# A hybrid mixer and mixture-of-experts block on one core: result rows ordered by expert index, and summed slot by slot

## The reference

```
def moe_ffn(h, w_router, b_router, w_gate_up, b_gate_up, w_down, b_down):
    logits = (hf @ w_router) + b_router
    top_logits, top_idx = lax.top_k(logits, TOP_K)      # 4 of 32 experts for each of 512 tokens
    top_w = jax.nn.softmax(top_logits, axis=-1)
    ...
    def expert_block(args):                             # gate/up, clamp, swiglu, down: a row of 1024 per choice
    ...
    y = jax.ops.segment_sum(ys * slot_w[:, None], slot_tok, num_segments=n_tok)
    return y
...
x = x + moe_ffn(h, ...)
return rmsnorm(x, norm_final_w)
```

## Time and profile before

| | us |
|---|---|
| median of 3 runs | 2107.06 |
| the three runs | 2105.13 to 2107.47 |
| the profiled execution | 2103.68 |
| its span in the trace | 2101.9 |
| PE busy | 1975.9 (94%) |
| DVE, ACT, POOL busy | 482.2, 329.9, 194.4 |
| granted TensorE clock, mean | 0.969 |

### The profile page before, as it was taken

The page is one execution under the profiler, slowest core; times in us unless marked ns, Lnnn a source line. Parts: engine busy times, 40 slices in busy tenths (PEclk is TensorE's granted clock), DMA queues, the critical chain, the costliest instruction groups (busy, mean ns, idle before and its releaser), DMA issues.

```text
span 2101.9 us, 42330 instructions
## 1 busy us (share of the span) xinstructions
PE 1975.9 (94%) x18196; PEld 899.5 (43%) x18196; DVE 482.2 (23%) x884; ACT 329.9 (16%) x614; POOL 194.4 (9%) x244
## 2 busy tenths in 40 slices
PE   6999999999999999957999999999999999999990
PEld 4445555455554444442434343434434343434340
DVE  1272553625522211220101010110101010110105
ACT  3122323323232000100001010100000010100001
POOL 0000010000100000030010111101010111101010
PEclk9999999999999999968999999999999999999995
DMA  6011111111102321346999999999999999999945
GB/s 248 20 41 46 41 56 31 41 46 41 41 21 104 108 84 64 130 166 233 379 386 391 378 386 390 383 397 377 395 380 394 381 396 381 392 392 380 391 170 216
DMA packets 77609, 488.61 MB, mean 232 GB/s; under 512 B 13780, under 2 KB 14312, under 8 KB 23232
## 3 DMA queue, kind: packets, MB, share of 16 engines
q1 hardware_dynamic: 68832, 470.76, 58.0%
q0 software_dynamic: 8704, 16.82, 2.4%
HBM read 478.53 MB, written 17.45 MB: 236 GB/s over the span
## 4 chain that ended last, share of the span: by engine, by line
PE 90%; DVE 5%; DMA 1%; issue 1%; DVEq 1%; ACT 1%; POOL 0%; SPq 0%; ACTq 0%; POOLq 0%
PE ps L968 31%; PE ps L525 17%; PE ps L986 16%; PE ps L520 15%; PE ps L733 2%; DVE arena L1358 2%; DVE arena L1355 2%; PE ps L997 1%; PE ps L953 1%; PE ps L963 1%; PE ps L979 1%; PE ps L845 1%; PE ps L840 1%; PE ps L820 0%; DMA arena<-expert_rows 0%
## 5 line engine op out<-in xcount | busy, mean ns | idle before, releaser
L968 PE MATMUL ps<-arena 128*32 128x512 f32 x6144 | 667.0, 594 | 0.0
L968 PEld LDWEIGHTS ps<-arena 128*32 128x32 f32 x6144 | 184.4, 110 | 464.6 <-issue 458.5
L525 PE MATMUL ps<-hT,arena 128*128 128x512 f32 x768 | 351.8, 601 | 7.9 <-DVE arena L1355 7.9
L986 PE MATMUL ps<-arena,hT 128*32 128x256 f32 x6144 | 338.1, 380 | 0.0
L1840 DVE TENSOR_SCALAR arena<-ps 128x768 f32<-128x768 f32 x32 | 30.6, 958 | 953.0 <-PE ps L968 953.0
L986 PEld LDWEIGHTS ps<-arena,hT 128*32 128x32 f32 x6144 | 184.8, 110 | 141.6 <-issue 1.1
L1037 ACT ACTIVATE arena<-ps 128x512 f32<-128x512 f32 (+4 forms) x144 | 87.5, 608 | 884.8 <-PE ps L953 696.7
L525 PEld LDWEIGHTS ps<-hT,arena 128*128 128x128 f32 x768 | 140.0, 192 | 154.8 <-issue 149.6
L1930 POOL DMA_INDIRECT expert_rows<-hT,six x96 | 95.8, 998 | 816.3 <-ACT hT L1037 769.3
L520 PE MATMUL ps<-arena 128*128 128x128 f32 (+3 forms) x480 | 142.0, 434 | 2.2 <-DVE arena L1355 2.2
L520 PEld LDWEIGHTS ps<-arena 128*128 128x128 f32 x480 | 77.4, 191 | 54.4 <-issue 47.1
(11 more groups left out here) (203 smaller groups left out, 1159.2 us busy)
## 6 DMA issues: line engine op xcount, KB each, us to landing
arena<-in_w_gu SPq DMA_DIRECT2D x256, 1024.0 KB, 7.9
arena<-in_w_dn SPq DMA_DIRECT2D x128, 1024.0 KB, 6.8
arena<-in_w_pair SPq DMA_DIRECT2D x16, 1024.0 KB, 4.9
arena<-in_w_merge SPq DMA_DIRECT2D x16, 1024.0 KB, 4.9
arena<-expert_rows SPq DMA_DIRECT2D x3, 2048.0 KB, 13.5
arena<-in_x SPq DMA_DIRECT2D x8, 512.0 KB, 6.4
arena<-in_w_qb SPq DMA_DIRECT2D x4, 768.0 KB, 4.3
arena<-in_w_cq SPq DMA_DIRECT2D x1, 2048.0 KB, 8.1
```

Of the source, the lines that this page charges most:

```text
L525: ins = pe.matmul(region(name)[:, cols], lhsT, rhs, start=(k == 0), stop=(k == n - 1))
L968: ins = pe.matmul(gu[32 * j:32 * (j + 1), g, :], xT[:, k, 32 * g:32 * (g + 1)], ring[k][:, 512 * j:512 * (j + 1)], start=False, stop=(k == ...
L986: ins = pe.matmul(yd[32 * j:32 * (j + 1), g, 0:256], aT[:, g, k, 32 * c:32 * (c + 1)], ring[8 + c][:, D * k + 256 * j:D * k + 256 * (j + 1 ...
```

## The change

A token's four slots are numbered by expert index in place of logit: slot 0 holds the lowest of the four experts. Slot 0 then lies among experts 0 to 28, slot 1 among 0 to 29, slot 2 among 0 to 30.

- **Routing.** `choose` computes for each of its two tiles the rank of each choice (how many of the four have a lower index), adds 4 x token (from four new columns of the constant `small`), and writes `valt`, which the host no longer gives. `choice_weights` puts the weights in the order of the ranks.
- **Start.** POOL clears 1024 columns of `oaT`; SP then fills all of `expert_rows` with zeros, four stores of 2 MB, issued behind the initial loads. DVE waits for them before its first write to `oaT`, POOL before the first gather.
- **End.** SP loads slot k of all four tiles (four loads of 512 KB) as soon as the scatters of experts 0 to 28 + k have landed and PE has used all up chunks, whose buffers the rows take, for k = 0, 1, 2. The norm's weights are loaded ahead of these. DVE adds the slots 0 to 2, slot by slot, in `acc` (the storage of `h2`, in `oaT`). Behind `all_rows` only slot 3 is loaded, and DVE adds one row in each tile before its norm.
- If `extra` is not zero, the three slots are loaded and summed again.

The diff, cut to its core:

```diff
@@ storage
-        yin = [ar(5 * b, 4 * D).rearrange("p (k d) -> p k d", k=TOPK) for b in range(NT)]
+        yin = [ar3(a, NT, D) for a in (16, 20, 8, 0)]
+        acc = h2
+        zero_rows = h2[:, 0, :]
@@ SP, start
-                             (wr[:, :, :], w_router), (br[:, :], b_router), (valt[:, :], ints[:, 0:16])):
+                             (wr[:, :, :], w_router), (br[:, :], b_router)):
...
+            sp.wait_ge(zero_set, 1)
+            for t in range(NT):
+                sp.dma_start(y_dram[t * P * TOPK:(t + 1) * P * TOPK, :].rearrange("(p k) d -> p k d", k=TOPK),
+                             zero_rows.unsqueeze(1).broadcast_to([P, TOPK, D])).then_inc(y_clear, 16)
@@ SP, end
+            sp.dma_start(nrow, norm_final.broadcast_to([P, D])).then_inc(row_in, 16)
...
+            sp.wait_ge(gu_used, 8 * NE)
+            for k in range(TOPK - 1):
+                sp.wait_ge(scattered, 16 * QUADS * (NE - TOPK + 1 + k))
+                for t in range(NT):
+                    sp.dma_start(yin[k][:, t, :], slot_rows(k, t)).then_inc(slot_in[k], 16)
             sp.wait_ge(list_done, 1)
...
             sp.wait_ge(all_rows, 1)
-            sp.dma_start(nrow, norm_final.broadcast_to([P, D])).then_inc(row_in, 16)
             for t in range(NT):
...
-                for k in range(TOPK):
-                    sp.dma_start(yin[t][:, k, :], rows_of_tile[:, k, :]).then_inc(last_y_in[k - 1] if k else rows_in[t], 16)
+                sp.dma_start(yin[TOPK - 1][:, t, :], slot_rows(TOPK - 1, t)).then_inc(rows_in[t], 16)
@@ DVE, first write to oaT
+                if i == 0 and g == 0:
+                    dv.wait_ge(y_clear, 16 * NT)
@@ DVE, choose(g)
+                for t in (2 * g, 2 * g + 1):
+                    order = pk[:, TOPK * t:TOPK * (t + 1), 0:TOPK]
+                    tt(order, ixf[:, t, :].unsqueeze(1).broadcast_to([P, TOPK, TOPK]), ixf[:, t, :].unsqueeze(2).broadcast_to([P, TOPK, TOPK]), ALU.is_lt)
+                    dv.drain()
+                    dv.tensor_reduce(rank[:, t, :], order, AXX, ALU.add)
+                    dv.drain()
+                    dv.tensor_scalar(valf[:, t, :], rank[:, t, :], sm[:, 89 + t:90 + t], None, ALU.add)
+                dv.drain()
+                dv.tensor_copy(valt[:, cs], valf[:, ts].rearrange("p t k -> p (t k)"))
@@ DVE, choice_weights()
-                tt(w4[:, :, :], e4[:, :, :], sum4[:, NT:2 * NT].unsqueeze(2).broadcast_to([P, NT, TOPK]))
+                tt(e4[:, :, :], e4[:, :, :], sum4[:, NT:2 * NT].unsqueeze(2).broadcast_to([P, NT, TOPK]))
+                by_rank = pk[:, :, 0:TOPK]
+                tt(by_rank, rank.rearrange("p t k -> p (t k)").unsqueeze(2).broadcast_to([P, 16, TOPK]),
+                   sm[:, 0:TOPK].unsqueeze(1).broadcast_to([P, 16, TOPK]), ALU.is_equal)
+                dv.drain()
+                tt(by_rank, by_rank, e4.rearrange("p t k -> p (t k)").unsqueeze(2).broadcast_to([P, 16, TOPK]))
+                dv.drain()
+                dv.tensor_reduce(w4[:, :, :], by_rank.rearrange("p (t k) r -> p t r k", t=NT), AXX, ALU.add)
@@ DVE, end
+            def add_rows(k, t):
+                src = acc if k else x2
+                stt(acc[:, t, :], yin[k][:, t, :], w4[:, t, k:k + 1], src[:, t, :], ALU.mult, ALU.add)
...
+            for k in range(TOPK - 1):
+                dv.wait_ge(slot_in[k], 16 * NT)
+                add_slot(k)
+                dv.sem_inc(early_sums, 1)
             extra = dv.value_load(lst[0:1, 2 * LIST:2 * LIST + 1], min_val=0, max_val=MAX_EXTRA)
...
             for t in range(NT):
                 dv.wait_ge(rows_in[t], 48)
-                for k in range(TOPK):
-                    if k and t == NT - 1:
-                        dv.wait_ge(last_y_in[k - 1], 16)
-                    stt(x2[:, t, :], yin[t][:, k, :], w4[:, t, k:k + 1], x2[:, t, :], ALU.mult, ALU.add)
-                    dv.drain()
+                add_rows(TOPK - 1, t)
                 dv.drain().then_inc(sum_done, 1)
@@ POOL
             po.memset(krp, 0.0).then_inc(zeroed, 1)
+            po.memset(zero_rows, 0.0).then_inc(zero_set, 1)
...
             po.wait_ge(tok_ready, 1)
+            po.wait_ge(y_clear, 16 * NT)
```

More of the change, by code:

```diff
@@ L333, in build @@
         at_done, aT_done, ys_done, six_done, scattered, all_rows = (sem(n) for n in ("at_done", "aT_done", "ys_done", "six_done", "scattered", "all_rows"))
-        last_y_in = [sem(f"last_y_in_{k}") for k in range(1, TOPK)]
+        slot_in = [sem(f"slot_in_{k}") for k in range(TOPK - 1)]
+        early_sums, again_in, zero_set, y_clear = sem("early_sums"), sem("again_in"), sem("zero_set"), sem("y_clear")
         sum_done, out_done, out_st = (sem(n) for n in ("sum_done", "out_done", "out_st"))
@@ L488, in _ @@
                         down_bias(j + NE, e)
+                sp.wait_ge(all_rows, 1)
+                for k in range(TOPK - 1):
+                    for t in range(NT):
+                        sp.dma_start(yin[k][:, t, :], slot_rows(k, t)).then_inc(again_in, 16)
             sp.wait_ge(all_rows, 1)
-            sp.dma_start(nrow, norm_final.broadcast_to([P, D])).then_inc(row_in, 16)
             for t in range(NT):
[L493 to L496, removed]
-                for k in range(TOPK):
-                    sp.dma_start(yin[t][:, k, :], rows_of_tile[:, k, :]).then_inc(last_y_in[k - 1] if k else rows_in[t], 16)
+                sp.dma_start(yin[TOPK - 1][:, t, :], slot_rows(TOPK - 1, t)).then_inc(rows_in[t], 16)
             for t in range(NT):
@@ L1346, in _ @@
                 ac.wait_ge(sum_done, t + 1)
-                ac.activation(junk, x2[:, t, :], ACT.Square, accum_out=r4[:, 0, t:t + 1])
+                ac.activation(junk, acc[:, t, :], ACT.Square, accum_out=r4[:, 0, t:t + 1])
                 ac.drain().then_inc(ss_done, 1)
@@ L1849, in _, with add_slot @@
                 expert(n)
+            def add_rows(k, t):
+                src = acc if k else x2
+                stt(acc[:, t, :], yin[k][:, t, :], w4[:, t, k:k + 1], src[:, t, :], ALU.mult, ALU.add)
+            def add_slot(k):
+                for t in range(NT):
+                    add_rows(k, t)
+                dv.drain()
+            for k in range(TOPK - 1):
+                dv.wait_ge(slot_in[k], 16 * NT)
+                add_slot(k)
+                dv.sem_inc(early_sums, 1)
             extra = dv.value_load(lst[0:1, 2 * LIST:2 * LIST + 1], min_val=0, max_val=MAX_EXTRA)
@@ L1854, in _ @@
                         expert(j + NE)
+                dv.wait_ge(again_in, 16 * NT * (TOPK - 1))
+                for k in range(TOPK - 1):
+                    add_slot(k)
             def finish(t):
@@ L1977, in constants @@
     small[:, 88] = np.arange(P) // 32
+    small[:, 89:89 + NT] = TOPK * (np.arange(P)[:, None] + P * np.arange(NT)[None, :])
     e, b = np.arange(NE)[:, None], np.arange(1, EXTRA + 1)
```

18 lines of the change are left out of this document (10 added, 8 removed).

## The result

| | before | changed |
|---|---|---|
| median, us | 2107.12 (4 runs, 2105.13 to 2107.47) | 2087.14 (4 runs, 2085.65 to 2089.16) |
| profiled execution, us | 2103.68 | 2086.33 |
| its span, us | 2101.9 | 2084.5 |

The ratio is 0.9911, with an interval of 0.9898 to 0.9924: 20.0 us less by the medians, 17.4 us by the spans of the two traces. The forecast was 2086.5 us. The time fell in the range, but in the trace the span is 3.2 us longer than the forecast's own sum gives: two of its steps were wrong, and the median hides that.

The account below looks back on a forecast made before the run. PE bounds 90% of the chain; only its idle end can move. 2064.1 + 14.2 + 3.0 gives a span of 2081.3, 20.6 us less, nothing elsewhere; from the median 2107.06, 2086.5 us, range 2083.5 to 2092.5.

Parts of the forecast that it names:

- What bounds the kernel, and the hole under the last down part: Chain 90% PE; only PE's idle end can move; early loads and additions fill idle DMA and DVE, saving 20.6 us.
- The arrival of slots 0 to 2: End, loads behind expert 31's down bias: slots land at 2046.1, 2051.1 and 2056.1, at 0.42 MB per us, without a gap.
- the late bound of 2045.1: End: latest landing forecast for expert 30's scatter, 2041.2 to 2045.1, before the DMA queue runs dry at about 2050.
- DVE ready for slot 3: End: three groups of four additions, 5.4 us each from 2046.1, then reading `extra` and branching; ready at 2063.3.
- `all_rows` stays at 2059.7: End: last scatter issued at 2056.4 after slot 2's load is over, so SP's first slot 3 load stays at 2059.7.
- the rival with the shared port: End: each of POOL's three scatter issues waits one whole 1.28 us addition; landing 3.8 us later, 2090.3 us; chance 0.26 with rival 1.
- rival 1: DMA queue is the new limit at the end: scatters share engines with loads, 1 to 6 us more; chance 0.26 with the port.
- The shared port: End, DVE additions beside POOL's preparation of expert 31's scatter: taken as free, by a row showing 0.97 us.
- the row at 979.25: Earlier trace row: an indirect DMA beside a two-SBUF-input addition took 0.97 us, like undisturbed ones; taken as showing no cost.
- Slot 3's load: End: first 512 KB load after 2059.7, bounds 2.6 and 4.4 us; 4.4 taken, landing at 2064.1.
- From there to the end: From slot 3's landing: 14.2 us to DVE's last result, table load now exposed, then 3.0 us to the span's end.
- Zero fill, routing, `valt`: Start and routing: fill over by 80 at the latest, small operations hidden in waits, one load gone; all taken as zero.

Follow-up runs that it names:

- the loads late: Changed kernel, but SP waits for all scatters of the experts before it loads slots 0 to 2; 2106.0 us, ratio 1.0001 to the kernel before.
- the loads early: Changed kernel with its early loads kept, but DVE waits for all scatters before its first early addition; 2098.6 us, ratio 0.9962.
- the bias first: Changed kernel, but the down bias of expert 31 is loaded ahead of its four down chunks, not behind; 2085.46 us, ratio 0.9901.
- the table ready: Changed kernel plus one spare square root on ACT ahead of its wait for the first summed tile, so the table loads early; 2087.8 us, ratio 0.9915.
- spare additions: Kernel with the loads late, plus six discarded DVE additions beside POOL's last scatter issues, before the row loads; measured once, 2105.71 us.
- slot 0 first: Changed kernel with slot 0 loaded ahead of expert 31's down chunks, its down bias before those chunks, norm weights during expert 1; 2082.35 us, ratio 0.9883.

## Why the prediction held, and where it did not

**What bounds the kernel, and the hole under the last down part.** Right. With the loads late, the gain is zero; with the loads early it is 7 us, with the additions early too 20.

**The arrival of slots 0 to 2.** Wrong by 3 us: they are added from 2049.2, 2054.2 and 2059.3, not 2046.1, 2051.1, 2056.1. The spacing of 5.05 us was right, and so was that the scatter of expert 30 leaves no gap, though it landed at 2046.2, a microsecond behind the late bound of 2045.1. The term that was mis-sized is the start: slot 0 takes 9.3 us behind the bias, not 6.2. The first 2 us of the rows' load run at 244 GB/s (2040 to 2042) where 415 follow; that is 0.8 us of the 3.1. The norm's 1.25 us were counted; the bytes of expert 30's scatter were not, and the last byte lies, by an estimate from the windows, more than a microsecond ahead of the addition. The rest of the difference is not taken apart. The rate of 0.42 MB per us is also a little above the 410 GB/s that the prediction names for it, which is 0.2 us. It cost nothing in the changed kernel, since DVE was ready at 2065.4 and slot 3 came at 2067.0; it is what held the kernel with the bias first.

**DVE ready for slot 3.** A group takes 4.9 us and not 5.4, since the drain between the additions is gone; the read of `extra` and the branch take 1.2, not 1.0. With the late start this gives 2065.4 for 2063.3.

**`all_rows` stays at 2059.7.** This is the step that failed: SP's issue came at 2062.93, 3.2 us later. The prediction named a sign of its own for it, a scatter of expert 31 that lands later than 2060; it landed at 2061.9. By that sign the account was wrong, although the time fell in the range. Its parts, against the earlier trace rows: PE ends 1.2 us later; the third issue begins 0.3 us later after the first (2.85 in place of 2.57); from there it is 3.99 us to the landing in place of 2.27, of which 1.05 is the longer issue and 0.7 the way to DRAM beside the end of slot 2's load. PE's part is the clock, which came back as late in two kernels without loads beside it. The other parts are the change's price, 2 us: a part of the rival with the shared port and of rival 1 came in. The 0.7 varies; the way from the end of the third issue to the landing is 1.3 us with no load beside it, 2.0 here, and 1.6 in each of the kernels without the fill and with the table ready. The 6 us at the upper end of rival 1 do not follow from its terms: the port and the late landing are 3.8 us each.

**The shared port.** I weighed the row at 979.25 against the rule and took the row: nothing. Here the additions cost 1.3 us over three issues, and 1.9 us in the kernel with spare additions and no loads; without additions all three were 0.98 to 0.99. My choice of a single row was the mistake. The blocking is of the kind that the Trainium skill gives, on its page "SBUF — State Buffer" in the rule on the shared port pair: the later instruction waits until the earlier one ends. The page says this of a GpSimd instruction that reads SBUF; whether the issue is held for that reason, no run here tells.

Why some issues pass shows when the single instructions of the changed kernel are listed (timeline, windows 2055.0 to 2055.2 and 2057.93 to 2058.0):

```profile
2054.20 1.28 DVE L1377 SCALAR_TENSOR_TENSOR oaT<-arena,w,oaT 128x1024 f32<-128x1024 f32 x1 [0.16 <-DMA arena<-expert_rows]
2055.08 1.26 POOL L1983 DMA_INDIRECT expert_rows<-hT,six  x1 [8.64 <-ACT hT L1056]
2057.83 1.27 DVE L1377 SCALAR_TENSOR_TENSOR oaT<-arena,w,oaT 128x1024 f32<-128x1024 f32 x1
2057.93 2.02 POOL L1983 DMA_INDIRECT expert_rows<-hT,six  x1 [0.30 <-issue]
```

The first issue ends 0.86 us after the addition that was under way when it began (2056.34 against 2055.48), the third 0.85 us after its own (2059.95 against 2059.10). In eight traces all 17 issues of over 0.98 us beside additions end 0.84 to 0.86 us after such an addition. The 11 that took 0.97 to 0.98 began at most 0.05 us after an addition had started, or just ahead of one, or in the last 0.04 us of one; one issue that began 0.05 us after (2057.48 of the spare additions) was held. The row at 979.25 is one of those that pass: its addition had started 0.02 us before, at 979.23. So an issue is held for the rest of the addition that it meets, and not, as the rival had it, for a whole one each. The price of three issues depends on how they fall between the additions: nothing with slot 0 first, 1.3 us here, 1.9 with the spare additions.

**Slot 3's load.** 4.0 us, where 4.4 was taken: right, within 0.4 us.

**From there to the end.** 14.5 + 3.1 us, where 14.2 + 3.0 was forecast. The table's way into the path was right, and so were the 3.3 us for each tile (2072.55, 2075.82).

**Sum.** A span of 2081.3 was forecast and is 2084.5: +3.2 for `all_rows`, -0.4 for the load, +0.3 behind it. From the profiled execution the forecast was 2083.1 us, and it is 2086.33. The median came within 0.6 us of the forecast because the profiled execution of before lay 3.4 us under its median and that of the changed kernel only 0.8: that is chance, not insight. As the traces of this study show, an execution gets or loses up to 4 us by PE's clock in the first 40 us.

**Zero fill, routing, `valt`.** Right. The fill moves 8.4 MB at 420 GB/s and is over by 60; the seven operations of `choose(1)` end 1.8 us before PE's count. Leaving the fill out changes nothing that the time can tell.

## What to carry to other kernels

When work is moved under another stage, sum the new neighbours and not only the hole: the moved additions and loads each delayed the one short operation that releases everything, the last scatter. A single row that shows two instructions side by side does not show that they leave each other alone: look at which of them was under way when the other began. After such a move two ways to the same point are close, so move the next item on both: moving the bias alone gave nothing that the time could tell, together with the first slot's load and the norm's weights 5 us. And forecast from the median, but check steps in the trace: a time that comes out right may be two errors and a lucky execution.

## What the runs showed of the hardware

- An indirect DMA of POOL takes 0.97 us to issue, and up to 2.07 us beside additions of 128 x 1024 on DVE with two inputs in SBUF; with the DMA engines idle, three issues took 4.81 us in place of 2.93. A held issue ends 0.84 to 0.86 us after the addition that was under way when it began (17 issues in eight traces); one that begins within about 0.05 us of the addition's start mostly passes.
- A scatter of three indirect DMAs lands 2.3 us after its third issue begins with nothing beside it, 3.5 us at the end of a stream of loads and 6.9 us in the midst of one (2053.04 to 2059.9), of which up to 1.1 is the longer issue.
- After a wait of 4 us PE's granted clock was 0.50 (1.2 GHz) and came back 2.8 to 5.7 us after the restart, in one and the same stretch of the program: 11.6 to 13.0 us for 192 matmuls in eight traces. Without that wait they took 10.55 us in two traces, with loads at 360 GB/s and more beside them, and 11.4 in a third. The late return came with DMA traffic and without it.
- The first 2 us of a load of the expert rows (pieces of 4 KB from DRAM) ran at 164 to 291 GB/s, with scatter traffic beside it or without, where some 400 follow.
